# Moving the converted-weight buffers by 64 bytes against the activations in SBUF

## What is computed

```python
def swiglu(x, wi, wo):
    gate, up = jnp.split(x @ wi, 2, axis=-1)
    return (jax.nn.silu(gate) * up) @ wo
for i in range(DEPTH):
    h = h + 0.5 * swiglu(rmsnorm(h, ln_ffn1[i]), ffn1_wi[i], ffn1_wo[i])
    h = h + mixer[i % 3](rmsnorm(h, ln_mix[i]))
    h = h + 0.5 * swiglu(rmsnorm(h, ln_ffn2[i]), ffn2_wi[i], ffn2_wo[i])
return rmsnorm(h, ln_final)
```

## Time and profile before

| | |
|---|---|
| median of three executions | 1952.17 us (1952.08 to 1952.53) |
| the profiled execution | 1952.87 us, its span 1951.1 us |
| mean granted TensorE clock | 0.998 |
| TensorE matmul (PE), weight load (PEld) | 99%, 85% of the span |
| VectorE, ScalarE, GpSimd | 70%, 58%, 3% of the span |
| DMA | 343.35 MB, mean 176 GB/s |

### The profile page before, as it was taken

One profiled execution on the slowest core, in us unless ns is written; L12 is line 12 of the kernel. 1 busy time (PEld: TensorE's weight loads), 2 busy tenths in 40 slices (PEclk: granted clock), 3 DMA queues, 4 the chain that ended last, 5 costly groups with the idle time before them and its releaser, 6 DMA issues.

```text
span 1951.1 us, 29477 instructions
## 1 busy us (share of the span) xinstructions
PE 1929.9 (99%) x10740; PEld 1666.6 (85%) x10754; DVE 1368.4 (70%) x1844; ACT 1129.1 (58%) x1678; POOL 64.6 (3%) x140
## 2 busy tenths in 40 slices
PE   8999999999999999999999999999999999999998
PEld 6888988888888888888888889888888888978887
DVE  6766676667876696676776776676677777767666
ACT  6555565555655566655565555765555556556553
POOL 2000000000100000000010001000000000000000
PEclk9999999999999999999999999999999999999999
DMA  6555534655555553455655544355556555535553
GB/s 220 193 192 194 173 130 134 212 193 191 163 193 188 172 195 130 157 192 190 215 173 193 190 159 123 130 173 193 193 173 208 187 188 171 173 117 167 191 193 119
DMA packets 244095, 343.35 MB, mean 176 GB/s; under 512 B 12077, under 2 KB 196026, under 8 KB 244026
## 3 DMA queue, kind: packets, MB, share of 16 engines
q1 hardware_dynamic: 242016, 340.29, 52.6%
q10 hardware_dynamic: 2010, 2.12, 0.5%
HBM read 340.27 MB, written 1.05 MB: 175 GB/s over the span
## 4 chain that ended last, share of the span: by engine, by line
PE 97%; DVE 1%; ACT 1%; DMA 0%; issue 0%; SPq 0%; ACTq 0%; POOL 0%; POOLq 0%; DVEq 0%
PE psum L528 35%; PE psum L691 33%; PE psum L699 17%; PE psum L986 5%; PE psum L1614 1%; PE psum L559 1%; PE psum L951 1%; PE psum L1028 1%; PE psum L1047 1%; PE psum L961 0%; DVE wlo L492 0%; ACT whi L473 0%; PE psum L1671 0%; DMA raw<-in_ffn_wi 0%; PE psum L1701 0%; PE psum L1578 0%
## 5 line engine op out<-in xcount | busy, mean ns | idle before, releaser
L473 ACT ACTIVATE whi<-raw,gains 128x512 fp32r<-128x512 f32 (+2 forms) x876 | 557.0, 709 | 270.7 <-PE psum L699 197.6
L691 PE MATMUL psum<-xT,whi 128*128 128x512 f32 x2816 | 678.9, 392 | 2.3 <-DVE wlo L512 1.9
L492 DVE SCALAR_TENSOR_TENSOR wlo<-raw,gains,whi 128x512 fp32r<-128x512 f32 (+2 forms) x876 | 597.0, 743 | 51.0 <-ACT whi L473 50.8
L691 PEld LDWEIGHTS psum<-xT,whi 128*128 128x128 f32 x2816 | 522.8, 189 | 111.2 <-issue 4.8
L699 PEld LDWEIGHTS psum<-xT,wlo 128*128 128x128 f32 x2816 | 349.5, 192 | 6.9
L699 PE MATMUL psum<-xT,wlo 128*128 128x256 f32 x2816 | 351.9, 283 | 0.0
L807 DVE TENSOR_TENSOR gate_in_T<-psum,low 128x512 f32<-128x512 f32 x88 | 60.9, 692 | 341.6 <-ACT low L754 340.9
L488 DVE TENSOR_TENSOR wlo<-raw,whi 128x2048 fp32r<-128x2048 f32 x100 | 228.5, 2285 | 45.6 <-ACT whi L469 45.6
L528 PE MATMUL psum<-whi,hidT_hi 128*128 128x512 f32 x640 | 249.0, 389 | 0.0
L528 PE MATMUL psum<-wlo,hidT_hi 128*128 128x512 f32 x640 | 249.0, 389 | 0.0
L528 PE MATMUL psum<-whi,hidT_lo 128*128 128x512 f32 x640 | 249.0, 389 | 0.0
(11 more groups left out here) (230 smaller groups left out, 1547.9 us busy)
## 6 DMA issues: line engine op xcount, KB each, us to landing
raw<-in_ffn_wi SPq DMA_DIRECT2D x350, 512.0 KB, 4.6
raw<-in_ffn_wo SPq DMA_DIRECT2D x176, 512.0 KB, 4.3
raw<-in_sb_w_in SPq DMA_DIRECT2D x48, 512.0 KB, 4.6
raw<-in_ml_w_in SPq DMA_DIRECT2D x24, 512.0 KB, 4.4
raw<-in_sb_w_out SPq DMA_DIRECT2D x16, 512.0 KB, 4.1
raw<-in_ml_w_out SPq DMA_DIRECT2D x8, 512.0 KB, 4.0
raw<-in_mla_w_out SPq DMA_DIRECT2D x8, 512.0 KB, 4.2
raw<-in_mla_w_in SPq DMA_DIRECT2D x4, 512.0 KB, 4.3
```

Source lines behind the costliest of these rows:

```text
L473: last = act.activation(whi[:, slot, r], raw[:, slot, r], ACT.Copy, scale=gain_col(p.gain + k))
L492: last = dve.scalar_tensor_tensor(wlo[:, slot, r], raw[:, slot, r], gain_col(p.gain + k), hi[:, r], op0=ALU.mult, op1=ALU.subtract)
L691: i = pe.matmul(psum[:, 4 + blk, :], whi[:, slot, k * 2 * FC + blk * P:k * 2 * FC + (blk + 1) * P], xT[:, 4 * part + k, :, :].rearrange("p ...
```

## The change

Only the order in which tensors are declared is changed. Tensors lie one behind the other in each partition in that order, each start rounded up to 32 bytes. No instruction, wait, queue, loop or size is changed; only addresses are.

```diff
         raw = sb("raw", [P, RING, PCOLS])
+        minus_half = sb("minus_half", [P, 16])
         whi = sb("whi", [P, RING, PCOLS], F32R)
         wlo = sb("wlo", [P, RING, PCOLS], F32R)
+        ssq = sb("ssq", [P, TT])
+        mean_sq = sb("mean_sq", [P, TT])
         h = sb("h", [P, TT, D])
         xT = sb("xT", [P, KD, 2, SEQ], F32R)
...
         neg_ones = sb("neg_ones", [P, P], F32R)
+        rstd = sb("rstd", [P, TT])
+        gate_bias = sb("gate_bias", [ML_HEADS, 2])
         sp_hi = sb("sp_hi", [P, 3 * NCOL], F32R)
         sp_lo = sb("sp_lo", [P, 3 * NCOL], F32R)
...
         mask = sb("mask", [P, 6, NCOL], BF16)
-        ssq = sb("ssq", [P, TT])
-        mean_sq = sb("mean_sq", [P, TT])
-        rstd = sb("rstd", [P, TT])
-        minus_half = sb("minus_half", [P, 16])
-        gate_bias = sb("gate_bias", [ML_HEADS, 2])
         pos_i = sb("pos_i", [P, TT], I32)
```

## The result

The changed kernel takes 1969.05 us (median of four, 1968.26 to 1969.61) against 1952.29 (1952.08 to 1952.53) for the kernel before, measured beside it: a ratio of 1.0084, interval 1.0071 to 1.0097. It is slower by 16.8 us. The forecast was 1927, the range 1884 to 1966: the time moved the other way and lies just outside the range.

The account below looks back on a forecast made before the run. TensorE was taken to bound the kernel, through its matmuls' start-to-start time. Savings of 7.4 + 5.6 + 12.5 = 25.5 us off the median of 1952.17 gave 1926.7, called 1927, range 1884 to 1966.

Parts of the forecast that it names:

- What bounds the kernel, and that only the step could move: Whole kernel: TensorE, busy 1929.9 of 1951.1 us; the change can act only through the time between matmul starts.
- That the step hangs on the distance of the two operands and repeats every 256 bytes: TensorE matmuls: start-to-start time depends on stationary-to-moving operand distance, repeating every 256 bytes or less; no size of its own.
- The rule weighed against it: TensorE's two SBUF read ports are independent, so distance can't matter and time stays at 1952; as a rival, 12%.
- Lines 699 and 986, 7.4 us less: 3680 narrow matmuls of 256 columns go from 119.7 to 117.7 ns each, 7.4 us less.
- Line 691, 5.6 us less: 2816 wide matmuls of 512 columns save the same 2.0 ns each as narrow ones, 5.6 us less.
- line 528, 12.5 us less: 2976 wide matmuls of 512 columns save 4.2 ns each, as taken from line 1648, 12.5 us less.
- The surplus: Time of a matmul beyond its columns: 13.4 ns for wide, 13.0 for narrow, so taken as independent of columns.
- The 4.2 ns for line 528: Saving per wide matmul there: 119.7 minus 115.5 ns, the latter a mean over four stretches of line 1648.
- the third: Wide matmuls of lines 691 and 528 never settle, 6.6 ns more each, 38 us, giving 1983; chance 18%.
- VectorE and ScalarE at nothing: Lines 492 and 488 keep their 746 and 2285 ns; these engines' work costs nothing more.
- small tensors at nothing: GpSimd, busy 64.6 us in all with operands of a few floats: moving these costs nothing.

Follow-up runs that it names:

- e1: Kernel before the change with only minus_half moved ahead of whi, so the rings and everything behind them move 64 bytes together: 1952.45 us, ratio 1.0.
- e2: Kernel before the change with only ssq and mean_sq moved ahead of h, so h, xT and hidden activations move 64 bytes, rings stay: 1969.62 us, ratio 1.0089.
- e3: Kernel before the change with a gap of 448 bytes between the rings and h: 1964.16 us, ratio 1.0064.
- e4: Kernel before the change with a gap of 256 bytes between the rings and h: 1952.33 us, ratio 1.0.
- e10: Kernel before the change with gaps of 64 bytes ahead of hid and 192 behind hidT_lo, displacing only the hidden activations: 1964.97 us, ratio 1.0065.
- e9: Kernel before the change with gaps of 192 bytes ahead of xT and 64 behind it, displacing only xT: 1949.26 us against 1952.41, ratio 0.9983.

## Why the prediction was wrong

- **What bounds the kernel, and that only the step could move:** right. The count, the waits and the other engines stayed, and all but some 2 us of the difference is in the steps of lines 528, 691, 699 and 986.
- **That the step hangs on the distance of the two operands and repeats every 256 bytes:** right, by e1, e2, e3, e4 and e10, but not the whole of it: at 64 and 192 one distance has two values. The rule weighed against it, that the two reads of TensorE are independent so that 1952 would stay, does not come true for these matmuls: of all that TensorE reads in line 528, e10 moves only the stationary operand, and each step grows by 6.6 ns.
- **Lines 699 and 986, 7.4 us less:** right. 119.7 to 117.8 ns where 117.7 was taken; 6.4 + 1.6 = 8.0 us over the traces.
- **Line 691, 5.6 us less, and line 528, 12.5 us less:** wrong in sign. These are the terms that failed, and they failed on one step: the saving of narrow matmuls was carried over to wide ones, because "the surplus was equal at both widths, so the same 2.0 ns". The surplus is 13.4 and 13.0 ns at distance 0, and that is a coincidence of distance 0. At 192 it is 20.0 ns wide, and 6.7 or 11.1 narrow. The price of a narrow matmul at a distance says nothing of a wide one there. Measured: line 691 costs 8.3 us, line 528 costs 12.8 in the chunks and 5.5 on `xT`. The 4.2 ns for line 528 had a second weakness: they came from a mean of 114.3 and 117.5 ns in line 1648, two values at one distance, which the mean hid.
- **The rival that came true** is the third, with its place (lines 691 and 528) and its marks: 5.60 us for line 528 in 78 of 80 groups, and 3.73 for line 691 in 40 of the 72 behind line 528. It was priced at 6.6 ns for all 5792 wide ones. Line 528 paid 6.6 in the chunks; line 691, at 64 and not 192, paid 2.5 or 6.2 behind line 528 and 1 ns behind line 699, and so the time is 1969 and not 1983. That its 6.6 ns was exact is luck. The three matmuls at 233.3 ns from which it was taken have their stationary operand `neg_tri` 1024 bytes before `sp_hi`, at distance 0 like lines 691 and 528, and such groups take 0.69 to 0.70 us before the change and after it, at distance 64: they are the start of a group, where line 691 at distance 0 has steps of 236, 228 and 233 ns too, and say nothing of another distance. No row before the change showed a wide matmul at another distance, so the sign was open, and the chance of a loss should have been higher than 18%.
- **VectorE and ScalarE at nothing, small tensors at nothing:** right; 746 and 2290 ns, and e1, which moves `minus_half`, is at 1.0.

What stays open: where in SBUF or in TensorE's read path the two operands meet, why a long sequence settles (comes to a constant or repeating step), and what picks one of its values and hands it on from chunk to chunk. The runs show the dependence on distance and width, and that there can be two values, not the circuit. Distances that are multiples of 16 and not of 32, with which a value better than e9's may be found, were not tried beyond 16 itself.

## What to carry to other kernels

In a kernel that TensorE bounds, the place of the moving operand against the stationary one in a partition is worth up to 1.8% (1952 against 1987 us here), and any small tensor declared between two large ones can shift it unseen. Read the step from start to start for each form of matmul, with its operands' distance, before and after such an edit, and read many groups, since one chunk can show the cheaper of two values; don't carry a step over from one width to another. Where a total stays put, look at the rows: a gain and a loss may have cancelled.

## What was not expected

- The step depends on the signed distance: wide matmuls at 64 run at 229.5 or 233.2 ns, at 192 only at 233.2, in either role. Narrow ones have 117.8 and 113.4 at both.
- The dependence is not smooth: 32 bytes cost as much as 192 for wide ones, and 8 bytes differ from 16 by 22 us in the whole kernel.
- A sequence can settle at more than one step at the same distance: line 699 at 192 takes 113.4 or 117.8 ns within e3, a whole SwiGLU at a time, and line 691 at 64 takes turns between 229.4 and 233.1 from chunk to chunk.
